# ScalarE's copy of turned probabilities ahead of the exponentials in half of the first attention's steps

## The chip, the cores and the metric

The kernel runs on one core of one Trainium2 chip. The metric is the device time of one execution in microseconds (us), as the median of several runs. One further execution was recorded by the hardware profiler; all rows below come from it. The engines are PE (TensorE, matrix products and transposes; PEld is its weight load), ACT (ScalarE), DVE (VectorE), POOL (GpSimd) and SP (the DMA queue's engine). PSUM is the memory of eight banks that PE writes and that ACT and DVE read.

## The reference

The program is three transformer blocks with 512 tokens and a width of 1024. Only the mixer of the first block is touched. It is an attention with three branches over shared queries (16 heads in 4 groups of 4): compressed, selected-block and window attention. With 512 tokens and 8 blocks of 64 the selection takes every block, and the window is 512, so the selected branch and the window branch are both plain causal attention, each with its own keys and values:

```python
o_cmp, p_cmp = compressed_attention(q, kcc, vcc)      # 31 compressed keys
sel_idx = select_blocks(p_cmp, S)
o_sel = selected_block_attention(q, ks, vs, sel_idx)  # softmax(q k^T / 8, causal) v
o_win = banded_attention(q, kw, vw, NSA_WINDOW, None) # the same with kw, vw
o = g[..., 0:1] * o_cmp + g[..., 1:2] * o_sel + g[..., 2:3] * o_win
return o.reshape(B, S, qd) @ w_out
```

Per head and branch the kernel computes scores of 512 queries against their causal keys, the maximum of a row, the exponential with its sum, the probabilities times gate over sum, their transposes, and the product with the values.

## The kernel before, in words

Every engine runs its own instruction stream, in the order in which the program text issues it, and waits on semaphores. The order around the change is written out by hand; no scheduler stands between.

A `Plan` object lists 36 **works** for the first attention (`PLAN_NSA`): nine for each group, namely heads 0 and 1 of branch 0, heads 0 and 1 of branch 1, one `cmp` work (the compressed branch of all four heads), then heads 2 and 3 of both branches. A work of a head is one head in one branch. Its scores lie in three PSUM banks, as four blocks of queries: block 3 (512 keys) in bank 0, block 2 (384) and block 0 (128) in bank 1, block 1 (256) in bank 2. There is one set of these banks, so the scores of the next work can only be written when the exponentials of this one have read them.

All engines step through t = 0, 1, 2 and so on, with a lag of two works (`LAG`). In step t:

- **PE** (`score`, `turn`, `value`) computes the scores of work t (L1090, and L1093 for the causal mask; L1075 for a `cmp` work), then transposes the finished probabilities of work t-2 (L1122; L1104 for `cmp`) into banks 3, 4 and 5, ten 128x128 pieces of which the first four fill bank 3, and then, if the plan lists one under `plan.after[t-2]`, computes a value product (L1150 for two works of one branch, L1133 for the compressed branch).
- **DVE** takes the negated row maxima of the four score blocks (`maxima`, L1859), computes 1/sum of the work before (`factor`, L1887), and copies banks 4 and 5 of the transposes to `pt` (L1902). In some steps it also adds up rows of the conditioning product (L1819).
- **ACT** computes the four exponentials of work t (`exponentials`, L2556: tile `pr` from `ps`, each followed by a short read of its accumulated sum), and copies bank 3 of the transposes of work t-2 to `pt` (`copy`, L2575; L2567 copies to `ptc` for a `cmp` work, L2545 is the exponential of a `cmp` work). After some steps it also takes the high part of a finished output (`high`, L2580).
- **POOL** multiplies the probabilities of work t-1 by gate and 1/sum (L812).

The waits that matter here: an exponential waits for the maxima of its bank (`nm_made`). The copy waits for PE's transposes into bank 3 (`p_turned`). The scores of work t+1 wait, bank by bank, for the exponentials of work t (`p_made`; `bank_read` in `score`). The transposes of work t-1 wait for the copies of work t-2 (`bank_copied`), for POOL's scaling of work t-1, and for nothing else.

`plan.after` holds a value product at 20 places. `plan.after.get(t - 1 - LAG)` is true when PE ended step t-1 with a value product, so that the scores of work t follow it. With works left to score, that is the case in the 18 steps t = 5, 7, 8, 10, 12, 14, 16, 17, 19, 21, 23, 25, 26, 28, 30, 32, 34 and 35. DVE already uses the same condition, to put its `factor` ahead of the maxima in these steps (L1920).

Before and after the first attention PE runs dense matrix products (L901 to L903). The second attention uses the same functions with another plan.

Of the kernel before, what the change touches and what calls it, by code (L numbers as in the profile page):

```python
# [203 lines left out]
LAG, EARLY = 2, 2  # L204
# [48 lines left out]
def build(nc, src, out):  # L253
# [42 lines left out]
    def small(name):  # L296
        a, b = COL[name]
        return sm[:, a:b]
# [294 lines left out]
    def pt_free(eng, plan, n):  # L593

        if n - plan.nth0 >= 4:
            eng.wait_ge(pv_made, plan.after_work(n - 4)[1])
        elif not plan.nsa and n - plan.nth0 < 2:
            eng.wait_ge(rot_made, 11)
        elif not plan.nsa:
            for index in (9, 10):  # L600
                eng.wait_ge(rot_kept[index % 2], rot_count(index))
# [1790 lines left out]
    def _(act):  # L2392
# [145 lines left out]
        def attention(plan, early=None):  # L2538
            works = plan.works

            def exponentials(w):
                g, kind, j = works[w]
                if kind == "cmp":
                    act.wait_ge(cmp_centred, g + 1)
                    a.activation(prc[:], prc[:], ACT.Exp).then_inc(p_made, 1)  # L2545
                    return
                n = plan.nth[w]
                s = n % 4
                if n - plan.nth0 >= 3:
                    act.wait_ge(p_turned, plan.after_work(n - 3)[0])  # L2550
                shift = st[:, 0 if plan.nsa else 3, s]
                for c, (i, b, col) in enumerate(plan.blocks):
                    act.wait_ge(nm_made, 4 * n + (plan.bank_end(c) + 1 if plan.nsa else 4))
                    k0, k1 = plan.keys(i)
                    width = (k1 - k0) * P
                    a.activation(pr[:, n % 3, b * S + col:b * S + col + width], ps[:, plan.s_bank(w, b), col:col + width],  # L2556
                                 ACT.Exp, bias=shift[:, i:i + 1], accum_out=st[:, 1, s, i:i + 1]).then_inc(p_made, 1)
                if not plan.nsa:
                    a.activation(st[:, 4, s], shift, ACT.Exp, bias=small("sinks")[:, 4 * g + j:4 * g + j + 1]).then_inc(p_made, 1)

            def copy(w):
                g, kind, j = works[w]
                if kind == "cmp":
                    act.wait_ge(p_turned, plan.turn[w][2])
                    if g:
                        act.wait_ge(pv_made, plan.valued((g - 1, "cmp", 1)))
                    a.copy(ptc[:], ps[:, plan.t_bank + 2]).then_inc(pt_act, 1)  # L2567
                    return
                n = plan.nth[w]
                for b, (engine, cols) in enumerate(plan.copies):  # L2570
                    if engine != "act":
                        continue
                    act.wait_ge(p_turned, plan.turn[w][b])
                    pt_free(act, plan, n)
                    a.copy(pt[:, n % 4, b * S:b * S + cols], ps[:, plan.t_bank + b, 0:cols]).then_inc(pt_act, 1)  # L2575

            def high(unit):
                c = plan.pair_of(unit)
                act.wait_ge(pv_made, plan.valued(unit))
                a.copy(ah[:, c], ps[:, 6 + c % 2]).then_inc(o_high, 1)  # L2580

            if early:
                for w in range(EARLY):
                    exponentials(w)
                return
            for t in range(0 if plan.nsa else EARLY, len(works) + LAG + 2):
                if t < len(works):
                    exponentials(t)
                if LAG <= t < len(works) + LAG:
                    copy(t - LAG)  # L2590
                for unit in plan.after.get(t - LAG - 1, ()):
                    if plan.is_last(unit):
                        high(unit)

        def mlp(name, b0, hid0):
# [3 lines left out]
            for b, (what, grp) in enumerate(MLP_BLOCKS):  # L2599
# [10 lines left out]
                u += DC  # L2610

        attention(PLAN_NSA)
        u = FIRST["nsa_out"]
        n = 20
# [9 lines left out]
        for p in range(4):  # L2624
            highs(u + RING + 2 + 2 * p, u + RING + 4 + 2 * p)
            rotated(7 + p, pair_s, query=True)
            if p == 2:
                attention(PLAN_SWA, early=True)
        highs(u + RING + 10, u + RING + 11)
        n += UNITS_SWA_IN  # L2630
        attention(PLAN_SWA)
        u = FIRST["swa_out"]
        highs_and_squares(u, y, n, factor=coef_at(1, 2))
# [265 lines left out]
```

## Time and profile before

| what | us |
|---|---|
| runs before: median (lowest to highest) of 3 | 2071.42 (2065.5 to 2071.64) |
| the profiled execution, its own time | 2069.99 |
| its span in the trace | 2068.2 |
| PE busy over the span | 1969.9 (95%) |
| ACT busy over the span | 695.6 (34%) |
| stretch of the first attention | about 181 to 350 |

The page's shares are means over the whole span. The first attention is a twelfth of it, so the rows below are from that stretch. In a row of the timeline the columns are start, duration, engine, line, operation, tile written and tiles read, size and count; in brackets stands how long the engine had been idle just before, and who ended that idle time.

### The profile page before, as it was taken

The numbers are of one execution on the slowest core, as the hardware profiler recorded it, in microseconds if no ns is written. First come the engines' busy times: TensorE is split into PE (matmuls) and PEld (weight loads), VectorE is DVE, ScalarE is ACT, GpSimd is POOL, SyncE is SP. The second block draws the span as 40 slices with busy tenths as digits, with TensorE's granted clock in tenths as the row PEclk, the third lists the DMA queues.
The fourth block names the chain that finished last, engine by engine and source line by source line (L and its number), as shares of the span: only waits on it lengthen the run. The fifth ranks groups of instructions, "written<-read, shape, count | busy, mean of one in ns | idle before, by whom it ended". The sixth has DMA issues, their size and how long they took to land.

```text
span 2068.2 us, 26747 instructions
## 1 busy us (share of the span) xinstructions
PE 1969.9 (95%) x10152; PEld 1616.7 (78%) x10152; DVE 1114.8 (54%) x1729; ACT 695.6 (34%) x1217; POOL 943.0 (46%) x552
## 2 busy tenths in 40 slices
PE   6999999999999999788999999999999999999997
PEld 5888776788888877667888888788897778888886
DVE  7576776864554667656422313676463338345163
ACT  3353564432222233544322213342343333222122
POOL 1465554465444445444444444543363335444442
PEclk9999999999999999999999999999999999999999
DMA  7775332455556415522333222222242123223231
GB/s 286 239 217 163 108 98 81 164 183 183 190 176 203 154 52 177 150 71 72 101 94 96 97 93 101 72 68 76 100 137 90 62 71 109 95 93 101 92 102 61
DMA packets 79986, 252.18 MB, mean 122 GB/s; under 512 B 12160, under 2 KB 12672, under 8 KB 79616
## 3 DMA queue, kind: packets, MB, share of 16 engines
q1 hardware_dynamic: 79872, 250.61, 37.3%
q8 instruction: 77, 1.26, 0.3%
q14 instruction: 37, 0.30, 0.0%
HBM read 235.21 MB, written 15.37 MB: 121 GB/s over the span
## 4 chain that ended last, share of the span: by engine, by line
PE 71%; issue 12%; POOL 7%; DVE 6%; ACT 3%; DMA 1%; SPq 0%; POOLq 0%; DVEq 0%; ACTq 0%
PE ps L901 19%; PE ps L903 19%; PE ps L902 19%; POOL wl L793 5%; PE ps L1150 2%; PE ps L1090 2%; PE ps L1122 2%; ACT pr L2556 1%; PE ps L1416 1%; DVE st L1859 1%; POOL al L849 1%; PE ps L1441 1%; PE ps L969 1%; POOL x L841 1%; PE ps L964 1%
## 5 line engine op out<-in xcount | busy, mean ns | idle before, releaser
L793 POOL TENSOR_TENSOR wl<-raw,wh 128x1024 fp32r<-128x1024 f32 x309 | 770.2, 2498 | 966.8 <-ACT wh L2411 966.7
L2411 ACT CAST wh<-raw 128x1024 fp32r<-128x1024 f32 x309 | 322.3, 1050 | 931.3 <-PE ps L903 854.7
L901 PE MATMUL ps<-ah,wh 128*128 128x512 f32 x1240 | 488.6, 394 | 1.5 <-DVE pair L1791 1.5
L902 PE MATMUL ps<-ah,wl 128*128 128x512 f32 x1240 | 483.4, 390 | 0.0
L903 PE MATMUL ps<-al,wh 128*128 128x512 f32 x1240 | 483.3, 390 | 0.0
L901 PEld LDWEIGHTS ps<-ah,wh 128*128 128x128 f32 x1240 | 233.2, 188 | 53.2 <-issue 3.0
L901 PE MATMUL ps<-hh,wh 128*128 128x512 f32 x688 | 271.0, 394 | 1.8 <-DVE hl L2368 1.7
L902 PEld LDWEIGHTS ps<-ah,wl 128*128 128x128 f32 x1240 | 233.3, 188 | 49.3 <-issue 1.5
L903 PEld LDWEIGHTS ps<-al,wh 128*128 128x128 f32 x1240 | 233.2, 188 | 49.2
L903 PE MATMUL ps<-hl,wh 128*128 128x512 f32 x688 | 269.9, 392 | 0.0
L902 PE MATMUL ps<-hh,wl 128*128 128x512 f32 x688 | 268.1, 390 | 0.0
L901 PEld LDWEIGHTS ps<-hh,wh 128*128 128x128 f32 x688 | 129.3, 188 | 30.5 <-DVE hl L2368 3.1
L903 PEld LDWEIGHTS ps<-hl,wh 128*128 128x128 f32 x688 | 129.2, 188 | 29.1
L902 PEld LDWEIGHTS ps<-hh,wl 128*128 128x128 f32 x688 | 129.2, 188 | 28.5
L2556 ACT ACTIVATE pr<-ps,st 128x512 f32<-128x512 f32 (+1 forms) x192 | 94.1, 504 | 75.3 <-DVE st L1859 42.2
L812 POOL TENSOR_SCALAR pr<-pr,st,gates 128x512 f32<-128x512 f32 (+3 forms) x128 | 81.0, 647 | 56.2 <-DVE st L1887 56.2
L2021 DVE TENSOR_SCALAR rs<-ps 128x512 f32<-128x512 f32 x64 | 44.2, 690 | 114.9 <-PE ps L903 109.9
L1090 PE MATMUL ps<-ks,qs 128*128 128x256 f32 (+3 forms) x384 | 89.4, 339 | 11.2 <-DMA qs<-qscr 6.4
L1859 DVE TENSOR_REDUCE st<-ps 128x1 f32<-128x512 f32 (+1 forms) x192 | 76.7, 449 | 28.5 <-PE ps L1093 16.5
L2034 DVE TENSOR_TENSOR y<-ps,y 128x512 f32<-128x512 f32 x32 | 22.1, 692 | 127.3 <-PE ps L903 127.3
L1997 DVE SCALAR_TENSOR_TENSOR acc_mlp<-ada_mlp,cond,acc_mlp 128x1024 f32<-128x1024 f32 x56 | 89.2, 1593 | 0.5
L1090 PEld LDWEIGHTS ps<-ks,qs 128*128 128x128 f32 x384 | 60.5, 195 | 22.8 <-issue 10.9
(373 smaller groups left out, 2806.8 us busy)
## 6 DMA issues: line engine op xcount, KB each, us to landing
raw<-in_units SPq DMA_DIRECT2D x309, 512.0 KB, 3.5
ada_mlp<-in_ada SPq DMA_DIRECT2D x64, 512.0 KB, 3.4
ada<-in_ada SPq DMA_DIRECT2D x16, 512.0 KB, 16.0
qs<-qscr SPq DMA_DIRECT2D x32, 256.0 KB, 3.7
ada_in<-in_ada SPq DMA_DIRECT2D x16, 512.0 KB, 3.6
ks<-kscr SPq DMA_DIRECT2D x24, 256.0 KB, 4.6
x<-in_xT SPq DMA_DIRECT2D x1, 2048.0 KB, 13.1
qscr<-rot_h SPq DMA_DIRECT2D x16, 128.0 KB, 2.4
```

The source lines that it names most:

```text
L793: nc.gpsimd.tensor_tensor(wl[:, slot], raw[:, slot], wh[:, slot].bitcast(F32), ALU.subtract).then_inc(lo_done, 1)
L812: op = nc.gpsimd.tensor_scalar(o, o, st[:, 2, n % 4, i:i + 1], gates[:, i, c:c + 1], ALU.mult, ALU.mult)
L901: nc.tensor.matmul(out_ap, wh[:, slot, k], high[:, k0 + k], start=first and k == 0, stop=False)
L902: nc.tensor.matmul(out_ap, wl[:, slot, k], high[:, k0 + k], start=False, stop=False)
L903: mm = nc.tensor.matmul(out_ap, wh[:, slot, k], low[:, k0 + k], start=False, stop=last and k == ks - 1)
L1090: nc.tensor.matmul(o, qs[:, Q_SLOT[j], i * P:(i + 1) * P], ks[:, slot, part, k0 * P:k1 * P], start=part == 0, stop=False)
L1122: mm = nc.tensor.transpose(ps[:, plan.t_bank + b, col + c * P:col + (c + 1) * P], pr[:, n % 3, at0:at0 + P], small("ident"))
L1859: op = v.tensor_reduce(st[:, 0, s, i:i + 1], ps[:, plan.s_bank(w, b), col:col + (k1 - k0) * P], X, ALU.max, negate=True)
L1997: op = v.scalar_tensor_tensor(out=a, in0=w, scalar=cond[:, n % 8:n % 8 + 1], in1=a, op0=ALU.mult, op1=ALU.add)
L2021: link(v.tensor_scalar(rs[:, k % 2], b, 0.0, None, ALU.max))
L2411: a.copy(wh[:, slot], raw[:, slot]).then_inc(hi_done, 1)
L2556: a.activation(pr[:, n % 3, b * S + col:b * S + col + width], ps[:, plan.s_bank(w, b), col:col + width], ACT.Exp, bias=shift[:, i:i + 1], ...
```

## The change

In the first attention, in the steps in which the scores of work t follow a value product on PE, ACT's copy of the turned probabilities of work t-2 is issued ahead of the four exponentials of work t. In all other steps, and in the second attention, it stays behind them. No instruction is added or removed, and no other engine's stream is changed.

```diff
             for t in range(0 if plan.nsa else EARLY, len(works) + LAG + 2):
+                copy_first = plan.nsa and bool(plan.after.get(t - 1 - LAG))
+                if copy_first and t < len(works) + LAG:
+                    copy(t - LAG)
                 if t < len(works):
                     exponentials(t)
-                if LAG <= t < len(works) + LAG:
+                if not copy_first and LAG <= t < len(works) + LAG:
                     copy(t - LAG)
```

The first place that moves is step 5, on ACT, right behind the exponential of the first `cmp` work (`prc`); `pr` is written by exponentials and `pt` by copies:

```order
 L2545 ACTIVATE prc<-prc 128x512
-L2575 COPY pt<-ps 128x512
-L2556 ACTIVATE pr,st<-ps,st 128x512
-L2556 ACTIVATE pr,st<-ps,st 128x384
-L2556 ACTIVATE pr,st<-ps,st 128x128
-L2556 ACTIVATE pr,st<-ps,st 128x256
-L2575 COPY pt<-ps 128x512
+L2575 COPY pt<-ps 128x512 x2
+L2556 ACTIVATE pr,st<-ps,st 128x512
+L2556 ACTIVATE pr,st<-ps,st 128x384
+L2556 ACTIVATE pr,st<-ps,st 128x128
+L2556 ACTIVATE pr,st<-ps,st 128x256
```

The copy of step 5 has moved up over its four exponentials and now stands directly behind the copy of step 4. Steps 7 and 8 on ACT before:

```order
64 L2567 COPY ptc<-ps 128x512
65 L2556 ACTIVATE pr,st<-ps,st 128x512
66 L2556 ACTIVATE pr,st<-ps,st 128x384
67 L2556 ACTIVATE pr,st<-ps,st 128x128
68 L2556 ACTIVATE pr,st<-ps,st 128x256
69 L2575 COPY pt<-ps 128x512
70 L2556 ACTIVATE pr,st<-ps,st 128x512
71 L2556 ACTIVATE pr,st<-ps,st 128x384
72 L2556 ACTIVATE pr,st<-ps,st 128x128
73 L2556 ACTIVATE pr,st<-ps,st 128x256
74 L2575 COPY pt<-ps 128x512
75 L2580 CAST ah<-ps 128x512
```

Each copy stands behind its step's exponentials. The same steps on ACT with the change:

```order
63 L2567 COPY ptc<-ps 128x512
64 L2575 COPY pt<-ps 128x512
65 L2556 ACTIVATE pr,st<-ps,st 128x512
66 L2556 ACTIVATE pr,st<-ps,st 128x384
67 L2556 ACTIVATE pr,st<-ps,st 128x128
68 L2556 ACTIVATE pr,st<-ps,st 128x256
69 L2575 COPY pt<-ps 128x512
70 L2556 ACTIVATE pr,st<-ps,st 128x512
71 L2556 ACTIVATE pr,st<-ps,st 128x384
72 L2556 ACTIVATE pr,st<-ps,st 128x128
73 L2556 ACTIVATE pr,st<-ps,st 128x256
74 L2580 CAST ah<-ps 128x512
```

Both copies stand ahead. PE's stream is the same in both kernels; this is its step 5, from the scores of work 5 to the first scores of work 6:

```order
732 L1090 MATMUL ps<-ks,qs 128x512 x2
733 L1093 MATMUL ps<-mask_r,ident_r 128x128
734 L1090 MATMUL ps<-ks,qs 128x384 x2
735 L1093 MATMUL ps<-mask_r,ident_r 128x128
736 L1090 MATMUL ps<-ks,qs 128x128 x2
737 L1093 MATMUL ps<-mask_r,ident_r 128x128
738 L1090 MATMUL ps<-ks,qs 128x256 x2
739 L1093 MATMUL ps<-mask_r,ident_r 128x128
740 L1122 MATMUL ps<-sm,pr 128x128 x10
741 L1090 MATMUL ps<-ks,qs 128x512 x2
```

The transposes for which the copy waits (L1122) stand behind all four score blocks of the work whose exponentials now stand behind the copy.

## Rows read from the trace of the kernel before

**Rows 1.** Busy time by window: start:end, length, busy of each engine, granted clock, DMA.
```profile
181.00:350.00 169.00, 157.11 (x1076) 121.97 (x1076) 127.36 (x280) 94.18 (x305) 90.71 (x137) 0.96 0.28 84
```

**Rows 2.** Timeline of steps 14 and 15: exponential on ACT; transposes, scores, transposes on PE.
```profile
246.97 0.69 ACT L2556 ACTIVATE pr<-ps,st 128x512 f32<-128x512 f32 x1 [1.98 <-DVE st L1859]
...
247.12 1.27 PE L1122 MATMUL ps<-sm,pr 128*128 128x128 f32 x10
248.15 0.70 PE L1090 MATMUL ps<-ks,qs 128*128 128x512 f32 x2
...
250.02 0.62 PE L1104 MATMUL ps<-sm,prc 128*128 128x128 f32 x4
```

**Rows 3.** Timeline of steps 23 and 24, ACT.
```profile
286.48 0.69 ACT L2556 ACTIVATE pr<-ps,st 128x512 f32<-128x512 f32 x1 [1.65 <-PE ps L1122]
...
287.71 0.36 ACT L2556 ACTIVATE pr<-ps,st 128x128 f32<-128x128 f32 x1
288.05 0.48 ACT L2556 ACTIVATE pr<-ps,st 128x256 f32<-128x256 f32 x1
288.50 0.60 ACT L2575 COPY pt<-ps 128x512 f32<-128x512 f32 x1
289.00 0.69 ACT L2556 ACTIVATE pr<-ps,st 128x512 f32<-128x512 f32 x1
```

**Rows 4.** Timeline of steps 23 and 24, PE.
```profile
285.33 1.27 PE L1122 MATMUL ps<-sm,pr 128*128 128x128 f32 x10
287.40 0.70 PE L1090 MATMUL ps<-ks,qs 128*128 128x512 f32 x2 [0.80 <-ACT pr L2556]
288.22 0.62 PE L1090 MATMUL ps<-ks,qs 128*128 128x384 f32 x2
...
289.41 0.61 PE L1104 MATMUL ps<-sm,prc 128*128 128x128 f32 x4
```

**Rows 5.** Timeline of the last steps: POOL, PE and ACT.
```profile
337.03 2.37 POOL L812 TENSOR_SCALAR pr<-pr,st,gates 128x512 f32<-128x512 f32 x4 [2.25 <-DVE st L1887]
...
340.99 1.28 PE L1122 MATMUL ps<-sm,pr 128*128 128x128 f32 x10 [1.47 <-ACT pt L2575]
...
341.65 0.59 ACT L2575 COPY pt<-ps 128x512 f32<-128x512 f32 x1 [0.32 <-PE ps L1122]
```

**Rows 6.** Timeline of steps 21 and 22 (`cmp` scores), PE and ACT.
```profile
275.97 1.27 PE L1122 MATMUL ps<-sm,pr 128*128 128x128 f32 x10
278.23 1.94 PE L1075 MATMUL ps<-kcs,qs 128*128 128x64 f32 x16 [0.99 <-ACT pr L2556]
...
277.52 0.47 ACT L2556 ACTIVATE pr<-ps,st 128x256 f32<-128x256 f32 x1
```

**Rows 7.** Timeline of steps 16 to 18: PE's transposes, and ACT's first exponential of 17.
```profile
254.66 1.27 PE L1122 MATMUL ps<-sm,pr 128*128 128x128 f32 x10
...
258.29 1.27 PE L1122 MATMUL ps<-sm,pr 128*128 128x128 f32 x10
...
261.65 1.27 PE L1122 MATMUL ps<-sm,pr 128*128 128x128 f32 x10
...
258.72 0.69 ACT L2556 ACTIVATE pr<-ps,st 128x512 f32<-128x512 f32 x1 [1.47 <-DVE st L1859]
```

**Rows 8.** Timeline of steps 26 and 27, PE (transposes, then scores 27).
```profile
297.68 1.05 PE L1122 MATMUL ps<-sm,pr 128*128 128x128 f32 x8
...
300.44 0.71 PE L1090 MATMUL ps<-ks,qs 128*128 128x512 f32 x2
```

**Rows 9.** Windows of 3 us behind two equal waits of PE (columns as Rows 1).
```profile
239.00:242.00 3.00, 3.00 (x22) 2.94 (x21) 1.56 (x3) 0.21 (x1) 1.93 (x4) 0.74 0.12 20
242.00:245.00 3.00, 3.00 (x14) 1.09 (x14) 2.66 (x6) 1.10 (x2) 1.05 (x1) 0.69 0.41 158
...
278.00:281.00 3.00, 2.77 (x25) 2.80 (x26) 2.12 (x5) 1.05 (x3) 1.54 (x3) 1.00 0.00 0
```

**Rows 10.** Who waited for whom, us 181 to 375: total us, times, longest.
```profile
PE ps L1075 <- ACT pr L2556: 5.2, 4, 2.3
```

## The prediction, made before the changed kernel was run

> **What bounds the kernel now.** I read first how busy each engine is in the stretch of the first attention: PE works 157.11 of 169 us there, DVE 127.36 and ACT 94.18 [rows 1]. PE sets the pace, and only 12 us of that stretch are PE waiting. So a change can give back a few of these 12 us, and anything that makes PE wait more is paid in full, since no other engine is near the bound. Next I read the timeline step by step, to see which wait ends last for PE. Behind a step with a value product PE runs scores of work t, the transposes of work t-2 and then at once the scores of work t+1, which need the banks that the exponentials of work t are reading. In step 14 the first exponential starts at 246.97, the transposes at 247.12, the next scores at 248.15 and the next transposes at 250.02 [rows 2]. In step 23, where ACT is later, PE waits 0.80 us for the exponentials [rows 4]. ScalarE's exponentials are thus on the edge of PE's path, while its copy is not: the only wait of PE for that copy that I find in the first attention is the 1.47 us near the end, ahead of the transposes of step 36 [rows 5].
>
> **The change, step by step.** I measure every step from T, the start of PE's transposes in it.
>
> How late do the exponentials get? The copy can start 0.66 us after T: transposes at 340.99, copy behind them at 341.65, with ACT idle until then [rows 5]. The next ACT instruction starts 0.50 us after a copy starts (288.50 to 289.00) [rows 3]. So the first exponential of a moved step starts at T + 1.16. Before, in step 14, it started at T - 0.15 (246.97 against 247.12) [rows 2], and the same, within 0.05 us, in fourteen of the eighteen steps (all but 8, 17, 23 and 32). That is 1.3 us later. The idle time that ACT had there (1.98 us [rows 2]) is no room for the copy, because it lies ahead of T: the transposes that the copy needs are queued on PE behind the very scores that the exponentials need.
>
> What does PE do? The first scores of work t+1 start 0.92 us after the first exponential (286.48, 287.40), those of the second bank 0.51 us after the third exponential starts (287.71, 288.22), and the next transposes 1.19 us after that (289.41) [rows 3, 4]. The third exponential starts 1.23 us after the first one [rows 3]. The exponential of the third bank comes 0.34 us behind (288.05) [rows 3] and does not bind. With the first exponential at T + 1.16 this puts the scores of work t+1 at T + 2.08, their second bank at T + 2.90, and the next transposes at T + 4.09.
>
> The eighteen steps fall into five kinds.
> - Steps 5, 10, 14, 19 and 28: the scores of a head follow at once. Before, the next transposes stood at T + 2.90 (247.12 to 250.02) [rows 2]. Loss 1.19 us each, 5.95 in all.
> - Steps 12, 21 and 30: the scores of the `cmp` work follow, and need all banks. They start 0.71 us after the fourth exponential starts (277.52, 278.23), before at T + 2.26 [rows 6]. Now the fourth exponential starts at T + 1.16 + 1.57 (286.48 to 288.05 [rows 3]) and the scores at T + 3.44. Loss 1.18 us each, 3.54 in all.
> - Steps 8 and 17: DVE is late, so the exponentials stood at T + 0.43 already (258.29, 258.72), and the next transposes at T + 3.36 (261.65) [rows 7]. Loss 0.73 us each, 1.46 in all.
> - Steps 7, 16 and 25: a short product of the compressed branch stands between, next transposes at T + 3.63 (254.66 to 258.29) [rows 7]. Loss 0.46 us each, 1.38 in all.
> - Steps 23, 26 and 32 lose nothing. In 23 and 32 the exponentials started at T + 1.15 anyway, behind the long chain of the `cmp` work (285.33, 286.48) [rows 3, 4]: the copy fits in front. In 26 sixteen more small matmuls stand among the transposes, and the next scores start only at T + 2.76 (297.68, 300.44) [rows 8].
>
> Steps 34 and 35 are the tail, where the copy is worth something. The transposes of step 36 waited 1.47 us for it and started at 340.99; now it is done by 340. But they also need POOL's scaling of the work, which ran from 337.03 for 2.37 us [rows 5] and hangs on exponentials that are 1.3 us later: it ends near 340.6. So of the 1.47 us about 0.3 come back, and later scaling is hidden by the value products that follow. The other side of the tail, that nothing comes back or all of it does, is 0 to 1.5 us.
>
> The losses add up, because PE has no wait further on that would swallow them: the waits that remain follow PE's own scores and move with them. DVE and POOL have slack. SP's loads, the second attention and everything behind 350 us only shift. The sum is 5.95 + 3.54 + 1.46 + 1.38 - 0.3 = 12.0 us.
>
> **The clock.** PE's longest repeated wait, ahead of the `cmp` scores, grows from 0.99 us [rows 6] to 2.2. Behind such a wait of 0.99 us the granted clock once fell, to means of 0.74 and 0.69 over two windows of 3 us; behind the equal wait 40 us later it stayed at 1.00 [rows 9]. A fall costs 3 x 0.26 + 3 x 0.31 = 1.7 us. The levels are 2.4 and 1.2 GHz, and what preceded the fall was a wait and then matmuls of 64 columns. With twice the wait I expect all three `cmp` steps to fall instead of one: two more, 3.4 us. The bounds are no more (0) and ten more, one for nearly each lengthened wait (17).
>
> The Trainium skill, on its page "TensorE: Matmul & The Clock Gate" (part 1, The HAM clock gate), says that the array's clock drops to half after PE has been idle and returns after sustained work. By that rule alone every one of the long waits is a candidate; by the rows one of two equal waits had a fall.
>
> Forecast: 2069.99 (the profiled execution's own time) + 12.0 + 3.4 = 2085.4. The median of the runs shown is 1.4 us above the profiled execution, and 2071.42 + 15.4 = 2086.8. I say 2086.
>
> **The rivals.**
> - Clock falls spread. With PE waiting 1 to 2 us in some thirteen steps, the clock falls behind most of them: ten more falls at 1.7 us. Time 2070 + 12 + 17 = 2099. Against it: behind the wait at 278.23 the clock held [rows 9], and the mean over the stretch is 0.96 [rows 1]. The page's rule gives this case.
> - Part of the loss is swallowed. If PE can run the first bank's scores of work t+1 early and only the second bank binds, or if DVE's share of the delay is made up in the next step, a step loses about half: 6 us, 2077. For it: in steps 15, 24 and the like ACT has idle time. Against it: that time lies behind PE's loss and cannot return it.
> - Not slower. In a moved step the exponentials do not start before T + 1.16 if DVE's first maximum ends later than that, as in steps 23 and 32 [rows 3, 4]. If DVE decides in most of the steps once the order changes, the copy is free everywhere, and the tail gives back up to 1.5 us: 2070 to 2072. It decides from the point at which the first maximum ends 1.1 us after T. In fourteen steps it ended 0.15 us or more ahead of T, so DVE would have to slip by 1.3 us with nothing in the change to make it.
> - That the change does not do what it says is excluded by the order on ACT, which moves as stated. A gain from earlier transposes is bounded by the one wait for a copy, 1.47 us [rows 5].
>
> **Chances.** A measurement of this kernel can tell about 0.3%, 6 us, from no change. Forecast (10 to 20 us more) 0.62, spreading clock falls (over 20) 0.13, partly swallowed (5 to 10) 0.17, not slower 0.08. Slower by over 0.3%: 0.62 + 0.13 + two thirds of 0.17 = 0.86; within 0.3%: the other third and three quarters of 0.08, 0.12; faster: 0.02, the rest. The range that leaves out 2 in 10 runs from 2077, the swallowed case, to 2095, some way into the spreading one.
>
> **What would show it.** In the changed profile, PE's wait for the exponentials ahead of L1075, 5.2 us in all [rows 10], grows by the 3.5 us of its three steps to 8.7, and that ahead of L1090 grows by about as much again or more. ACT shows idle time ahead of the copy, ended by PE's transposes, in about fifteen steps, and none ahead of the exponentials there. The wait of 1.47 us near the end is gone. The last value product of the first attention starts some 12 to 15 us later, and everything behind keeps its length. Granted clock below 1 behind each `cmp` score confirms the second term. I am wrong if PE's busy share in the stretch stays at 93%, or if exponentials in steps 10, 14 and 19 start before their step's transposes.

## The result, and the profile after

The changed kernel takes 2088.69 us (median of 4 runs, 2087.88 to 2090.33), the kernel before 2070.68 (median of 4). The ratio is 1.0093, with a 95% interval of 1.0075 to 1.0111: slower by 18 us, where 2086 was forecast, inside the range of 2077 to 2095. The profiled execution took 2088.05 us, its span is 2086.3 us where it was 2068.2.

All of it arises by the end of the first attention. Its last value product started at 347.71 us before and starts at 366.10 us now, 18.4 us later, and what follows it is as long as before to 0.3 us.

First the waits between 181 and 375 us of the changed kernel (who waited for whom: us in total, times, longest):

```profile
ACT pt L2575 <- PE ps L1122: 56.3, 19, 5.1
...
ACT pr L2556 <- DVE st L1859: 11.1, 18, 3.1
PE ps L1090 <- ACT pr L2556: 10.1, 11, 1.6
...
PE ps L1075 <- ACT pr L2556: 8.4, 4, 2.2
```

ACT's idle time has changed its cause: it waited 42 us for DVE's maxima ahead of the exponentials, and now waits 56 us for PE's transposes ahead of the copy. PE waits for exponentials 8.4 us ahead of the `cmp` scores, where it was 5.2 [rows 10], and 10.1 us ahead of the others, where it was 3.6.

Step 14 of the changed kernel on its timeline, the answer to [rows 2]:

```profile
254.10 0.59 ACT L2575 COPY pt<-ps 128x512 f32<-128x512 f32 x1 [3.03 <-PE ps L1122]
254.59 0.69 ACT L2556 ACTIVATE pr<-ps,st 128x512 f32<-128x512 f32 x1
...
253.45 1.27 PE L1122 MATMUL ps<-sm,pr 128*128 128x128 f32 x10
255.52 0.70 PE L1090 MATMUL ps<-ks,qs 128*128 128x512 f32 x2 [0.79 <-ACT pr L2556]
256.34 0.62 PE L1090 MATMUL ps<-ks,qs 128*128 128x384 f32 x2
...
257.54 0.62 PE L1104 MATMUL ps<-sm,prc 128*128 128x128 f32 x4
```

With T = 253.45 the copy starts at T + 0.65, the first exponential at T + 1.14, the next scores at T + 2.07 and the next transposes at T + 4.09. The prediction had T + 0.66, 1.16, 2.08 and 4.09.

The long wait is the one ahead of a `cmp` score, here in step 21 (answers to [rows 6]):

```profile
285.82 1.27 PE L1122 MATMUL ps<-sm,pr 128*128 128x128 f32 x10
289.25 1.94 PE L1075 MATMUL ps<-kcs,qs 128*128 128x64 f32 x16 [2.16 <-ACT pr L2556]
```

From T to the `cmp` scores it is 3.43 us, where it was 2.26. The granted clock behind the three of them, by windows of 3 us (columns as in [rows 9]):

```profile
242.00:245.00 3.00, 1.90 (x11) 1.93 (x11) 0.18 (x1) 1.44 (x7) 1.73 (x3) 0.73 0.03 5
245.00:248.00 3.00, 3.00 (x16) 3.00 (x17) 1.47 (x3) 0.00 (x0) 0.65 (x2) 0.50 0.16 33
248.00:251.00 3.00, 3.00 (x13) 1.11 (x14) 2.66 (x6) 1.03 (x2) 1.05 (x1) 0.63 0.38 145
...
290.00:293.00 3.00, 3.00 (x21) 2.91 (x20) 1.70 (x3) 0.00 (x0) 1.79 (x4) 0.70 0.18 50
293.00:296.00 3.00, 3.00 (x17) 1.20 (x16) 2.66 (x6) 1.10 (x2) 1.05 (x1) 0.73 0.35 125
...
335.00:338.00 3.00, 3.00 (x19) 3.00 (x19) 1.34 (x2) 0.00 (x0) 1.76 (x4) 0.59 0.02 5
338.00:341.00 3.00, 3.00 (x10) 1.17 (x10) 2.63 (x7) 0.86 (x2) 1.05 (x1) 0.50 0.00 0
341.00:344.00 3.00, 3.00 (x19) 1.94 (x16) 1.43 (x5) 0.24 (x1) 1.05 (x1) 0.77 0.00 0
```

Three slow stretches, in which the granted clock is at half (1.2 of 2.4 GHz), stand behind these scores where one was before, and the first and the third last twice as long. (A further one lies behind the `cmp` scores of step 4, in both profiles: from 196.1 to 202.9 us before, from 199.0 to 202.4 now.) The tail, POOL and PE, against [rows 5]:

```profile
356.92 2.37 POOL L812 TENSOR_SCALAR pr<-pr,st,gates 128x512 f32<-128x512 f32 x4 [3.42 <-DVE st L1887]
...
357.40 1.27 PE L1122 MATMUL ps<-sm,pr 128*128 128x128 f32 x10
359.35 1.31 PE L1122 MATMUL ps<-sm,pr 128*128 128x128 f32 x10 [0.68 <-POOL pr L812]
...
366.10 2.38 PE L1150 MATMUL ps<-pt,vv 128*64 128x512 f32 x16 [0.98 <-DVE pt L1902]
```

The wait of 1.47 us for the copy is gone, and a wait of 0.68 us for POOL stands in its place.

The starts of PE's transposes, read off both timelines step by step, give the account of the 18.39 us:

| term | predicted us | measured us |
|---|---|---|
| steps 5, 10, 14, 19, 28 | 5 x 1.19 = 5.95 | 5 x 1.17 = 5.86 |
| waits of steps 12, 21, 30 | 3 x 1.18 = 3.54 | 3 x 1.17 = 3.52 |
| steps 8, 17 | 2 x 0.73 = 1.46 | 0.69 + 0.72 = 1.41 |
| steps 7, 16, 25 | 3 x 0.46 = 1.38 | 0.41 + 0.45 + 0.43 = 1.29 |
| steps 23, 26, 32 | 0 | 0 |
| tail, steps 34 and 35 | -0.3 | 0.43 - 0.79 = -0.36 |
| slow clock behind the `cmp` scores, beyond before's | 3.4 | 1.6 + 1.6 + 3.3 = 6.5 |
| where step 5 began | 0 | 0.1 |

The term of the clock is taken from the times between transposes: in the changed kernel the three stretches cost 3.3, 1.6 and 3.3 us, the one before cost 1.6.

### The profile page after: what moved, and what is told of

It reads as the page before. It is cut to its first block, busy times and chain, and to the rows that moved or that the text cites. A ratio compares the mean times of both kernels' runs of the same rounds, so it can differ in the third digit from the quotient of the medians.

```text
span 2086.3 us, 26747 instructions
## 1 busy us (share of the span) xinstructions
PE 1977.3 (95%) x10152; PEld 1619.7 (78%) x10152; DVE 1116.6 (54%) x1729; ACT 694.9 (33%) x1217; POOL 940.3 (45%) x552
## 4 chain that ended last, share of the span: by engine, by line
PE 71%; issue 12%; POOL 7%; DVE 5%; ACT 4%; DMA 0%; SPq 0%; POOLq 0%; DVEq 0%; ACTq 0%
PE ps L901 19%; PE ps L903 19%; PE ps L902 19%; POOL wl L793 5%; PE ps L1150 3%; PE ps L1090 2%; ACT pr L2556 2%; PE ps L1122 2%; PE ps L1416 1%; POOL al L849 1%; PE ps L1441 1%; POOL x L841 1%; PE ps L969 1%; PE ps L949 0%; PE ps L964 0%
## 5 line engine op out<-in xcount | busy, mean ns | idle before, releaser
L1090 PE MATMUL ps<-ks,qs 128*128 128x256 f32 (+3 forms) x384 | 88.8, 335 | 16.6 <-ACT pr L2556 10.1
```

The lines of the kernel that those rows point to most:

```text
L1090: nc.tensor.matmul(o, qs[:, Q_SLOT[j], i * P:(i + 1) * P], ks[:, slot, part, k0 * P:k1 * P], start=part == 0, stop=False)
```

## The experiments

The kernels of each batch ran beside the kernel before on one chip; its median moved between 2069.40 and 2071.28 us from batch to batch, so kernels are compared by their ratios. My theory: the exponentials wait behind the copy, the copy waits for transposes that PE issues behind the scores, so PE's next scores come late; and the long waits ahead of the `cmp` scores bring the clock down. The rivals: it is ScalarE work ahead of the exponentials that costs, or the clock falls for another reason.

**Waiting or working.** Two kernels split the copy into its wait and its work, each ahead of the exponentials in the 18 steps, with the real copy behind them as before.

```diff
+                if plan.nsa and bool(plan.after.get(t - 1 - LAG)) and t < len(works):
+                    act.wait_ge(p_turned, plan.turn[t - LAG][0])
                 if t < len(works):
                     exponentials(t)
```

> In the 18 steps ACT only waits for PE's transposes into bank 3 ahead of the exponentials; the copy stays behind them. My theory splits the 1.3 us of delay into 0.8 us of waiting and 0.5 us of copying. It expects first exponentials at T + 0.66, losses of 0.69 us in steps 5, 10, 14, 19 and 28, of 0.68 in 12, 21 and 30, of 0.23 in 8 and 17, none in 7, 16 and 25, and 0.6 at the tail, 6.5 us in all, and on top 0 to 6 us of slow clock behind the cmp scores: 2077 to 2083. The rival that it is the copy's own ScalarE time in front of the exponentials expects next to nothing: 2071.

Measured: 2077.39 us, ratio 1.0026 (1.0009 to 1.0043). Step 8 of this kernel on the timeline:

```profile
218.33 0.69 ACT L2556 ACTIVATE pr<-ps,st 128x512 f32<-128x512 f32 x1 [1.01 <-PE ps L1122]
...
217.68 1.27 PE L1122 MATMUL ps<-sm,pr 128*128 128x128 f32 x10
219.26 0.70 PE L1090 MATMUL ps<-ks,qs 128*128 128x512 f32 x2 [0.31 <-ACT pr L2556]
```

The first exponential starts at T + 0.65. By the timeline steps 5, 10, 19 and 28 lose 0.69 us each, 12, 21 and 30 lose 0.68, 8 and 17 lose 0.2, and the tail 0.7. The waiting alone makes some 0.7 of the 1.17 us.

The other kernel does the work without the wait (the line is shortened here; two scratch tiles take turns):

```diff
+                if plan.nsa and bool(plan.after.get(t - 1 - LAG)) and t < len(works):
+                    a.copy(scratch, small("cmp_add"))
                 if t < len(works):
                     exponentials(t)
```

> In the 18 steps ACT does an additional copy of 128x512 elements that waits for nothing (it writes a scratch tile) ahead of the exponentials; the real copy stays behind them. My theory expects no change (2069 to 2073), since ACT idles 0.75 us or more there and the additional 0.5 us fit. The rival, that more ScalarE work in front of the exponentials is what costs, expects 0.5 us in each of 13 steps, 6.5 us: 2077.

Measured: 2070.43 us, ratio 0.9997 (0.9986 to 1.0008): no difference. Step 14 of it (its line numbers are one higher):

```profile
245.67 0.62 ACT L2589 COPY spare<-sm 128x512 f32<-128x512 f32 x1
...
247.67 0.69 ACT L2557 ACTIVATE pr<-ps,st 128x512 f32<-128x512 f32 x1 [1.38 <-DVE st L1860]
...
247.84 1.27 PE L1123 MATMUL ps<-sm,pr 128*128 128x128 f32 x10
```

As much ScalarE work (0.62 us, read from SBUF where the real copy reads PSUM) that waits for nothing lies inside ACT's idle time, and the first exponential stays at T - 0.17. From step 5 to the last product every interval of PE's transposes is within 0.1 us of before. So it is not work in front that costs but work that waits. Only because of that wait do the copy's 0.5 us fall behind T and count too.

**Kinds of steps.** The copy first in one kind of step alone:

```diff
+                copy_first = plan.nsa and t in (5, 10, 14, 19, 28)
```

> The copy stands first in steps 5, 10, 14, 19 and 28 alone, where the scores of a head follow at once. My theory expects 5 x 1.17 = 5.9 us at 350 us and PE waits of 0.79 us in these steps, about 2077, and no slow clock in them beyond what before shows behind the cmp scores. The rival, that part of each delay is made up by the next step (which other moved steps hid), expects some 3 us: 2074.

Measured: 2075.91 us, ratio 1.0023 (1.0014 to 1.0032). The time alone lies between the 5.9 us of my theory and the 3 us of the rival. The timeline decides: the five steps lose 1.17 us each, and no other step gives any back. This refutes the rival of the prediction by which part of the loss is swallowed.

```diff
+                copy_first = plan.nsa and t in (12, 21, 30)
```

> The copy stands first in steps 12, 21 and 30 alone. My theory expects 3 x 1.17 = 3.5 us of longer waits (2.16 us each by the waits ahead of the cmp scores), and slow clock behind each of the three, 3 to 6.5 us more than before, so 2077 to 2081. The rival that many waits bring the clock down expects 3.5 us and one slow stretch, as before: 2074.

Measured: 2077.01 us, ratio 1.0031 (1.0019 to 1.0042), for three waits that are 1.17 us longer: more than their 3.5 us. Slow stretches stand behind the first and the third, none behind the second. Behind the third, the timeline shows something new: PE's transposes of step 32 come 1.63 us late by the slow clock, and those of step 33 come 1.17 us of it early again.

> The copy stands first in all steps of the change but 12, 21 and 30, whose next scores are those of a cmp work. My theory (each moved step costs the delay of the exponentials that PE's next scores show, and the long waits ahead of the cmp scores bring the clock down for 6.5 us more than before) expects, at 350 us, 11.7 - 3 x 1.17 = 8.2 us more than before, with one slow stretch behind a cmp score as before (0 to 2 us either way), so a time of about 2079. The rival that the clock falls because PE waits more in many steps expects slow stretches behind all three cmp scores still, 6.5 us more than before in clock alone, and about 2085.

That kernel leaves out 12, 21 and 30 from the change. Measured: 2079.04 us, ratio 1.0041 (1.0026 to 1.0055), as expected. By the timeline 8.2 us are lost in the moved steps and 1.6 us in a slow stretch behind the third `cmp` score, although its wait was as short as before.

**The steps that I had put down at nothing.**

```diff
+                copy_first = plan.nsa and bool(plan.after.get(t - 1 - LAG)) and t < len(works) and t not in (23, 26, 32)
```

> The change without steps 23, 26 and 32, which I had put down at nothing. At full clock they cost nothing. But in the steps behind a cmp work the exponentials wait for the cmp chain of DVE and POOL, and PE then has some 1.2 us of slack behind its transposes. Where the clock was slow in front of them, PE arrives late and this slack swallows 1.2 us of it, unless the copy stands first and ties the exponentials to PE. New theory: 1.2 us less in each of 23 and 32 behind a slow stretch, 2.3 us less than the changed kernel with three slow stretches: 2086. The prediction's own view (nothing) expects 2089.

Measured: 2083.39 us, ratio 1.0065 (1.0050 to 1.0079), where the whole change has 1.0093 (1.0075 to 1.0111) and its repeat further on 1.0089 (1.0068 to 1.0109). These intervals overlap, so the timeline has to tell. Step 23, behind a slow stretch (ACT, then PE):

```profile
295.73 0.69 ACT L2556 ACTIVATE pr<-ps,st 128x512 f32<-128x512 f32 x1 [3.11 <-DVE st L1859]
...
295.89 1.27 PE L1122 MATMUL ps<-sm,pr 128*128 128x128 f32 x10
...
296.91 0.70 PE L1090 MATMUL ps<-ks,qs 128*128 128x512 f32 x2
...
298.80 0.61 PE L1104 MATMUL ps<-sm,prc 128*128 128x128 f32 x4
```

The exponential starts ahead of the transposes, and from them to the next transposes it is 2.91 us, not 4.08 as in [rows 4]: 1.17 us of the slow stretch are taken back, in step 23 and again in step 32. With the copy in front neither step can do that.

Then the same must hold for steps 5 and 14, which also stand right behind a `cmp` work. It does. Before, both stood behind a slow stretch, and took 2.91 and 2.90 us. Step 14 where none stood ahead of it and the copy was not moved there, in the profile of step 35 alone (further on; ACT, then PE):

```profile
246.73 0.69 ACT L2556 ACTIVATE pr<-ps,st 128x512 f32<-128x512 f32 x1 [1.65 <-PE ps L1122]
...
245.58 1.27 PE L1122 MATMUL ps<-sm,pr 128*128 128x128 f32 x10
...
249.67 0.61 PE L1104 MATMUL ps<-sm,prc 128*128 128x128 f32 x4
```

The exponential starts at T + 1.15 and the next transposes at T + 4.09. The bracket, like that of step 23 in [rows 3], names PE's transposes, but by the program text the exponential waits for transposes of an earlier step only, long done, and for DVE's first maximum: DVE starts that at 245.96, right behind its part of the `cmp` work. In seven profiles no slow stretch stood ahead of step 14. In six of them it took 4.1 us, 1.2 more than before, whether the copy was moved (this kernel, the filling in the change) or not (the filling before, the filling with step 35, step 35 alone, the wait alone); in the seventh, with the copy behind the first exponential, it took 4.6. Step 5 took 4.38 us in the three profiles without a slow stretch ahead of it (12, 21 and 30 alone, the filling with step 35, the filling in the change), again moved or not. So steps 5, 14, 23 and 32 are one kind. The copy in front costs them nothing at full clock, and 1.17 us behind a slow stretch. Only 10, 19 and 28 cost 1.17 us always.

The rest of the difference in time, 5 us from the change (4 from its repeat) where 23 and 32 explain 2.3, is not explained: the times of this kernel spread over 8 us. Its profile has no slow stretch ahead of step 14; whether its other runs also have fewer was not shown.

**What brings the clock down.** Into the wait ahead of each `cmp` score PE gets matmuls whose result is overwritten, into score bank 0, which the exponentials have read by then:

```diff
                 if kind == "cmp":
+                    pe.wait_ge(p_made, plan.expd[w - 1][0])
+                    for _ in range(4):
+                        nc.tensor.matmul(ps[:, 0], qs[:, Q_SLOT[works[w - 1][2]], 3 * P:4 * P],
+                                         ks[:, plan.k_slot(g, 1), 0, 0:S], start=True, stop=True)
```

> The changed kernel, with four additional matmuls of 512 columns of PE into score bank 0 (read out by then) ahead of each cmp score, inside the long wait; their results are overwritten. My theory says that idleness ahead of the small cmp matmuls brings the clock down: it expects the cmp scores to start as in the changed kernel, and at most one slow stretch instead of three behind them, 3 to 6 us less than the changed kernel: 2083 to 2086. The rival, that the small matmuls of the cmp scores or something else bring it down, expects the same slow stretches: 2089.

Measured, on top of the change: 2081.77 us, ratio 1.0054 (1.0039 to 1.0069), some 7 us less than the change and 5 less than its repeat. In its profile the first slow stretch is gone, the second and third remain. Of the wait of 2.16 us 0.97 are still idle there, 0.70 of them ahead of the filling, which can't start before the first exponential has read its bank. So this alone leaves the cause half open.

> The kernel before, with three additional matmuls of 512 columns into bank 0 in the wait ahead of each cmp score. If idleness there brings the clock down, the slow stretches behind the first cmp score (about 3 us lost) and behind the second (1.6 us lost) go, and it is 2 to 4 us faster than before: 2067 to 2069. If not, it is equal or up to 1 us slower, since the three matmuls take 0.93 us of a wait of 1.2.

The same with three matmuls in the kernel before: 2067.71 us, ratio 0.9984 (0.9974 to 0.9994). No slow stretch stands behind the `cmp` scores of steps 13, 22 and 31, though one remains behind the first `cmp` scores, in step 4. The profile doesn't show where the 3 us went: its first attention, from the first transposes to the last product, took 159.3 us, before it was 159.0, and what is shorter lies behind it (1715.0 us for 1720.5), where the filling adds nothing.

**How much of the delay each exponential brings.** The copy behind the first of the four exponentials:

```diff
                                  ACT.Exp, bias=shift[:, i:i + 1], accum_out=st[:, 1, s, i:i + 1]).then_inc(p_made, 1)
+                    if c == 0 and meanwhile:
+                        meanwhile()
```

> In the 18 steps the copy stands behind the first of the four exponentials instead of ahead of all. My theory: the first exponential keeps its time, and the second starts at T + 1.16 instead of T + 0.65, so that the second bank of PE's next scores binds at T + 2.22 and the loss is 0.5 us where it was 1.17 (steps 5, 10, 12, 14, 19, 21, 28, 30), 0.5 in 8 and 17 and behind the cmp chain in 23 and 32, none in 7, 16, 25 and 26, and 1.0 us comes back at the tail: 5 us at 350 us, 0 to 4 more by the clock, 2075 to 2080. The rival that any copy ahead of the later exponentials costs the whole delay expects the time of the change, 2088.

Measured: 2076.24 us, ratio 1.0030 (1.0020 to 1.0041). By the timeline 5, 10, 12, 19, 21 and 28 lose 0.5 us each, 8 and 17 0.44 and 0.49, and the tail gives 1.0 back. In step 10 PE's next scores start into the first bank without a wait, and those of the second bank at T + 2.22, behind a wait of 0.42 us: here the later exponentials bound PE, as the working said.

> The changed kernel once more, beside the others on one chip. If three slow stretches behind the cmp scores are its rule, the profile shows them again and the time is 2088 to 2090; if they were chance, steps lose the same 11.7 us and the clock term is anything from 0 to 6.5 us: 2082 to 2089.

The change once more: 2087.12 us, ratio 1.0089 (1.0068 to 1.0109). Its steps lose the same as in the table within 0.05 us. All three slow stretches are there. They cost 3.3, 1.6 and 1.6 us, 4.9 beyond that of before, where it was 6.5. The time lies just under the 2088 to 2090 that was expected with three of them. In the profiled execution (2084.55 us) the first attention is as long as in the first profile (176.3 and 176.5 us); the 3.5 us by which it is shorter lie behind it.

**A version that should beat both.** Step 35 has no scores behind it:

```diff
+                copy_first = plan.nsa and t == 35
```

> The copy stands first in step 35 alone, where no scores follow. My theory expects the transposes of step 36 1.4 us earlier relative to those of step 35, since nothing delays POOL's scaling of that work, and the last value product 1.1 us earlier, then bounded by POOL's scaling of the last work: 2070, 0.05% less, which the times can hardly tell but the trace can. The rival, that the last work's late exponentials take all of it back, expects 0.

Measured: 2068.96 us, ratio 0.9995 (0.9986 to 1.0005), not told from no change by the time. The timeline shows it:

```profile
337.89 2.71 PE L1122 MATMUL ps<-sm,pr 128*128 128x128 f32 x20
...
346.20 2.38 PE L1150 MATMUL ps<-pt,vv 128*64 128x512 f32 x16 [0.99 <-DVE pt L1902]
```

The transposes of steps 35 and 36 now run without a break. Taken from step 35's, the last product starts 8.31 us later, where it was 9.46 (338.25 to 347.71): 1.15 us less.

> The version that should beat both kernels: the kernel before with the three filling matmuls ahead of each cmp score and the copy first in step 35 alone. The filling gave 3.6 us (0.9984), step 35 should give 1.1 more: 2066 to 2067.

Both together: 2066.83 us, ratio 0.9989 (0.9979 to 0.9999), faster than the kernel before by an interval that just leaves out 1. The time is the expected one, the gain is not: the kernel before took 2069.40 us in this batch, so it is 2.6 us, by the ratio 2.3, and not 4.7. The times don't tell this kernel from the filling alone. PE in step 12, and a window that answers to [rows 9]:

```profile
234.50 1.28 PE L1126 MATMUL ps<-sm,pr 128*128 128x128 f32 x10
235.53 0.94 PE L1071 MATMUL ps<-ks,qs 128*128 128x512 f32 x3
236.77 1.94 PE L1079 MATMUL ps<-kcs,qs 128*128 128x64 f32 x16 [0.29 <-ACT pr L2560]
...
239.00:242.00 3.00, 3.00 (x24) 1.67 (x22) 2.90 (x7) 0.00 (x0) 1.14 (x2) 1.00 0.53 175
181.00:350.00 169.00, 157.94 (x1102) 122.13 (x1103) 127.36 (x284) 94.63 (x306) 91.48 (x137) 1.00 0.28 88
```

The wait is 0.29 us instead of 0.99, and the granted clock is 1.00 over the whole stretch, where it was 0.96 [rows 1]. From the first transposes to the last product it is 155.6 us here, where it was 159.0.

Over the profiles, the `cmp` scores of steps 13, 22 and 31 (each behind its wait) had a slow stretch so often:

| wait ahead of the scores | kernels | slow stretches |
|---|---|---|
| 0.99 us filled to 0.3 | filling before, filling with step 35 | 0 of 6 |
| 0.99 us | before, and the four that leave 12, 21, 30 alone | 5 of 15 |
| 1.5 to 1.7 us | wait alone, copy behind the first exponential | 3 of 6 |
| 2.16 us | change (twice), 12, 21, 30 alone, without 23, 26, 32 | 10 of 12 |
| 2.16 us, partly filled | filling in the change | 2 of 3 |

The `cmp` scores of step 4, behind a wait of 1.6 to 2.3 us where it is not filled, had one in 10 of 11 such profiles and in 1 of the 3 with the filling. Longer idle waits and slow stretches go together, then. That idleness is the cause was shown in part only: 0 of 6 and 5 of 15 could differ by chance, and a version without the small matmuls of 64 columns behind the waits was not run.

## Why the prediction was right

What bounds the kernel: right. PE set the pace, ACT's exponentials stood at the edge of its path, and the copy did not.

How late the exponentials get: right to 0.02 us, and the sum of the five kinds and the tail came to 11.7 us where 12.0 was worked out. Each was computed from durations between rows of the trace before, and was met because the order and the operations stayed the same and one dependency moved. The wait kernel and the work kernel show that it is that dependency. The signs came as stated: PE's wait ahead of L1075 went from 5.2 to 8.4 us (8.7 was worked out), PE's busy share in the stretch fell from 93% to 88%, and no moved step's exponentials start before T + 1.13. One did not: the last product came 18.4 us later, not 12 to 15, and what is over is the clock.

The tail: right in size (-0.36 us for -0.3) and in cause: POOL's scaling, itself delayed by the exponentials, took the copy's place as the last wait.

The clock: right in direction and in the number of slow stretches, but the term was mis-sized, 6.5 us and in the repeat 4.9 us where 3.4 stood. The failed step is the price of 1.7 us for a fall. It was read off one stretch, and two of the three in the changed profile took nearly twice that. The number three was in part luck: of the twelve waits of 2.16 us ten had a slow stretch, and two of the four kernels had only two.

The grouping of the steps was wrong in part, though the sum hid it. "Steps 23, 26 and 32 lose nothing" holds at full clock alone, and steps 5 and 14 belong with 23 and 32, not with 10, 19 and 28. The prediction took step 14 as its pattern [rows 2], and that step stands right behind the slow stretch of [rows 9]: that is why its exponentials started at T - 0.15 and not, as in step 23, at T + 1.15. The loss of 1.17 us in steps 5 and 14 is slack that used to swallow a slow stretch. For the same reason "PE has no wait further on that would swallow them" was wrong: there is 1.2 us behind each `cmp` work, which swallows what PE loses between the `cmp` scores and the next step, as long as the copy doesn't stand first there. The change lost this four times, 4.7 us. The forecast held 2.4 of it under steps 5 and 14. The rest stands in the table within the 6.5 us of the clock, since before no slow stretch stood ahead of 23 and 32: with the copy unmoved there, 2.3 of these 6.5 us would have come back.

The rivals: that the copy is free everywhere, and that losses are swallowed in half, are both refuted, the first by the exponentials' starts and the second by the five steps alone. Falls behind most of the thirteen waits did not come: behind the waits of 0.79 us in steps 5, 10, 14, 19 and 28 no slow stretch stood in either profile of the change. The Trainium skill ("TensorE: Matmul & The Clock Gate", part 1) says that the clock gate follows how busy PE has been recently; the table of slow stretches by length of wait agrees in direction, 0 of 6 at 0.3 us against 10 of 12 at 2.16.

## What to carry to other kernels

On an engine that works in order, ask of a step that is moved ahead what it waits for, not how long it takes: 0.6 us of work that waited for nothing was free in idle time, and the mere wait cost 0.7 us in each of seven steps. Here PE, the engine that sets the pace, issued the transposes behind the very scores whose exponentials now stood behind the copy. So PE paid the delay in full. Move a copy ahead only where nothing behind it feeds the bound, as in the last step. And before a step serves as the pattern for others, look whether it stands at full clock.

## What was not expected of the hardware

Three useless matmuls (0.94 us) in each wait of TensorE ahead of the `cmp` scores made the kernel 0.16% faster by the times (0.9984, 0.9974 to 0.9994), though its own profile doesn't show the gain in the first attention. The profile of the filling with step 35, where no slow stretch is left, does: 1.8 us less from the transposes of step 3 to those of step 6, and 0.4 us less in steps 13 and 14. Slow stretches came in sizes of about 1.6 us lost or twice that. And equal waits did not have equal effects: the same 0.99 us had a slow stretch in 5 cases of 15, so one profile does not price a wait that is followed by small matmuls. A fall of 1.6 us cost only 0.4 to 0.5 us net where an unmoved step behind it had its slack.
